# Row sums by half tiles, an early second expert tile, and group loads on the weights' queue, in a streaming-encoder block with a product-key expert layer

## What is computed

```python
qry = (xt @ w_query).reshape(TOKEN_BLOCK, PEER_HEADS, 2, PEER_HALF)
s1 = einsum('thd,hnd->thn', qry[:, :, 0], sub_keys1); s2 = ...   # top 16 of each, then top 16 of their sums
gate = softmax(top_s, axis=-1)
u, vv = expert_down[idx], expert_up[idx]
pre = einsum('td,thkd->thk', xt, u)
act = gelu(pre) * gate
out = einsum('thk,thkd->td', act, vv)
```

## Time and profile before

| | us |
|---|---|
| median of 3 runs | 3568.76 (3567.64 to 3570.26) |
| profiled execution, its own time | 3564.6 |
| its span | 3562.8 |
| TensorE busy (matmuls) | 3507.9, 98% |
| TensorE's weight loads busy | 3183.2, 89% |
| VectorE busy | 2171.1, 61% |
| ScalarE busy | 1413.8, 40% |
| POOL busy | 2045.6, 57% |

### The profile page before, as it was taken

One profiled execution on the slowest core, in us unless ns is written; L12 is line 12 of the kernel. 1 busy time (PEld: TensorE's weight loads), 2 busy tenths in 40 slices (PEclk: granted clock), 3 DMA queues, 4 the chain that ended last, 5 costly groups with the idle time before them and its releaser, 6 DMA issues.

```text
span 3562.8 us, 50874 instructions
## 1 busy us (share of the span) xinstructions
PE 3507.9 (98%) x20053; PEld 3183.2 (89%) x20053; DVE 2171.1 (61%) x3773; ACT 1413.8 (40%) x1780; POOL 2045.6 (57%) x718
## 2 busy tenths in 40 slices
PE   7999999999999999999999999999999999999999
PEld 5777777777788888898999999999999999999999
DVE  6333434343685137897676767443577777777774
ACT  5544545555422223323444444433333333333332
POOL 2333333333344434377666667687777777777774
PEclk9999999999999999999999999999999999999999
DMA  4322222222344332288999898999999999999994
GB/s 153 134 105 101 94 88 96 83 99 85 119 142 180 119 114 95 92 312 347 346 364 350 345 366 348 355 380 385 379 375 370 361 373 365 387 371 366 370 368 167
DMA packets 184738, 895.04 MB, mean 251 GB/s; under 512 B 15720, under 2 KB 69224, under 8 KB 90600
## 3 DMA queue, kind: packets, MB, share of 16 engines
q1 hardware_dynamic: 59232, 399.47, 30.1%
q0 software_dynamic: 49392, 359.68, 25.5%
q10 hardware_dynamic: 75928, 133.30, 10.2%
HBM read 828.39 MB, written 69.21 MB: 252 GB/s over the span
## 4 chain that ended last, share of the span: by engine, by line
PE 59%; issue 22%; DVE 8%; POOL 6%; DMA 3%; ACT 1%; DVEq 0%; ACTq 0%; POOLq 0%; SPq 0%
PE ps L1524 56%; DVE ps L1309 6%; POOL w_lo L350 5%; PE ps L1754 2%; DMA expert_rows<-down_rows,idx 1%; DVE h_dense L1442 1%; DMA w_e_raw<-w_stream 1%; POOL w_e_lo L357 1%; DVE expert_rows L1296 0%; PE ps L1688 0%; DMA g_dram<-gate_buf 0%; DVE hn_lo L1139 0%; POOL expert_rows L385 0%; ACTq L847 0%; ACT w_e_hi L724 0%
## 5 line engine op out<-in xcount | busy, mean ns | idle before, releaser
L357 POOL TENSOR_TENSOR w_e_lo<-w_e_raw,w_e_hi 128x2048 fp32r<-128x2048 f32 x256 | 1184.5, 4628 | 476.4 <-ACT w_e_hi L724 474.9
L350 POOL TENSOR_TENSOR w_lo<-w_raw,w_hi 128x2048 fp32r<-128x2048 f32 x115 | 536.6, 4666 | 934.2 <-ACT w_hi L417 934.2
L1524 PE MATMUL ps<-sn_hi,w_e_hi 128*128 128x344 f32 x2048 | 664.2, 324 | 11.4 <-POOL w_e_lo L357 8.7
L1524 PE MATMUL ps<-act_hi,w_e_hi 128*128 128x344 f32 x2048 | 658.4, 321 | 11.4 <-DVE h_dense L1442 11.4
L1524 PE MATMUL ps<-sn_lo,w_e_hi 128*128 128x344 f32 x2048 | 655.3, 320 | 0.0
L1524 PE MATMUL ps<-act_hi,w_e_lo 128*128 128x344 f32 x2048 | 655.2, 320 | 0.0
L1524 PE MATMUL ps<-sn_hi,w_e_lo 128*128 128x344 f32 x2048 | 654.1, 319 | 0.0
L1524 PE MATMUL ps<-act_lo,w_e_hi 128*128 128x344 f32 x2048 | 651.5, 318 | 0.0
L724 ACT ACTIVATE w_e_hi<-w_e_raw 128x2048 fp32r<-128x2048 f32 x256 | 489.2, 1911 | 191.3 <-DMA w_e_raw<-w_stream 106.6
L1296 DVE SCALAR_TENSOR_TENSOR expert_rows<-expert_rows,ps 128x2048 f32<-128x2048 f32 x171 | 388.3, 2282 | 259.7 <-DMA expert_rows<-down_rows,idx 143.2
L1524 PE MATMUL ps<-xn_hi,w_hi 128*128 128x512 f32 x1088 | 447.2, 411 | 18.7 <-DVE xn_lo L927 18.7
(11 more groups left out here) (260 smaller groups left out, 4853.7 us busy)
## 6 DMA issues: line engine op xcount, KB each, us to landing
w_e_raw<-w_stream SPq DMA_DIRECT2D x256, 1024.0 KB
w_raw<-w_stream SPq DMA_DIRECT2D x116, 1024.0 KB, 4.8
gel_dram<-gel_all ACTq DMA_DIRECT2D x32, 704.0 KB
g_dram<-gate_buf ACTq DMA_DIRECT2D x11, 2048.0 KB
gel_in<-gel_dram ACTq DMA_DIRECT2D x32, 704.0 KB
g_exp<-g_dram ACTq DMA_DIRECT2D x32, 704.0 KB
gate_dram<-g_raw ACTq DMA_DIRECT2D x32, 256.0 KB, 2.0
g_in<-gate_dram ACTq DMA_DIRECT2D x16, 512.0 KB, 5.8
```

The source lines that it names most:

```text
L350: nc.gpsimd.tensor_tensor(wlo[s][:, :], raw[s][:, :], whi[s][:, :].bitcast(F32), ALU.subtract).then_inc(lo_ready, 1)
L357: nc.gpsimd.tensor_tensor(e_lo[j % 4][:, :], e_raw[j % 4][:, :], e_hi[j % 3][:, :].bitcast(F32), ALU.subtract).then_inc(lo_ready, 1)
L1524: m = mm(ps[:, bank, 0:width], lhs[:, w], r, start=(n % (3 * per) == 0), stop=(n % (3 * per) == 3 * per - 1))
```

## The change

1. `FIRST_USED` gets six other numbers.
2. Items are placed by half tiles (`ITEM_HALF`); the tile of each item is as before. VectorE does a tile's rows in two places, one for each half; in the up stage each quarter of a group has the same order, and the fourth low part comes behind the row of that quarter's first half.
3. `peer_hi(1)` moves right behind `peer_hi(0)`, ahead of the last but one query block's key scores; `query_out` of the last block moves between the ninth and tenth `scaled_hi`; POOL waits for all of `sn_lo` before `low(1)` and not behind `low(2)`.
4. `gates(n)` and `gates_out(n)` stand a tile later, `one_hots(n)` where it was.
5. `load_group` of groups 2 to 31 moves from ScalarE's queue to SP's, behind the load of tile 4g + 3 of each group.

```diff
-FIRST_USED = [5, 9, 11, 14, 16, 18]
+FIRST_USED = [6, 10, 13, 16, 19, 21]
...
-ITEM_TILE = [T_GATES + (i - FIRST_ROWS) * DOT_TILES // (ADD_X - FIRST_ROWS) if i < ADD_X
-             else T_ACT + 1 + (i - ADD_X) * ADD_TILES // (N_ITEMS - ADD_X)
+ITEM_HALF = [2 * T_GATES + (i - FIRST_ROWS) * 2 * DOT_TILES // (ADD_X - FIRST_ROWS) if i < ADD_X
+             else 2 * T_ACT + 2 + (i - ADD_X) * 2 * ADD_TILES // (N_ITEMS - ADD_X)
              for i in range(FIRST_ROWS, N_ITEMS)]
+ITEM_TILE = [k // 2 for k in ITEM_HALF]
...
+            sp_view = g_dram.rearrange("g p (k c) -> p g k c", c=4 * GT)
+
+            def load_group(g):
+
+                s = slot_of(g)
+                sp.wait_ge(gel_out[g % 2], 16 * (g // 2 + 1))
+                sp.wait_ge(up_in[s], 32 * (loads_of(g) - 1))
+                sp.dma_start(gel_in[s][:, :], gel_dram[g]).then_inc(up_in[s], 16)
+                sp.dma_start(g_exp[s][:, :].rearrange("p (g c) -> p g c", g=GATE_GROUPS),
+                             sp_view[:, :, bass.ds(g, 1), :].rearrange("p g k c -> p (g k) c")).then_inc(up_in[s], 16)
+
             for j in range(2 * EXPERT_TILES):
                 load_experts(j)
+                g = (j - EXPERT_TILES - 3) // 4
+                if j >= EXPERT_TILES and j % 4 == 3 and g + 2 < GROUPS:
+                    sp.wait_ge(a_lo, 4 * g + 4)
+                    load_group(g + 2)
...
             for t in range(2 * EXPERT_TILES):
+                if t == 0:
+                    pool.wait_ge(slo_ready, CT)
                 if t + 1 < 2 * EXPERT_TILES:
                     low(t + 1)
                 if t == 1:
                     pool.wait_ge(idx3_ready, 1)
-                    pool.wait_ge(slo_ready, CT)
...
                     if isinstance(t, int) and t == CT - 2:
                         peer_hi(0)
+                        peer_hi(1)
...
             key_out(CT - 2)
-            peer_hi(1)
             for c in range(CT):
                 scaled_hi(c)
-            query_out(CT - 1, 1)
+                if c == CT // 2:
+                    query_out(CT - 1, 1)
             key_out(CT - 1)
...
-                    if GATE_TILE[n] == t:
+                    if GATE_TILE[n] + 1 == t:
                         gates_out(n)
...
-                    if g + 2 < GROUPS:
-                        if g:
-                            act.wait_ge(a_lo, 4 * g + 4)
-                        load_group(g + 2)
...
-            def rows_of_tile(t):
+            def rows_of_half(k):
                 for i in range(FIRST_ROWS, N_ITEMS):
-                    if tile_of(i) == t and i != TURN_X:
+                    if ITEM_HALF[i - FIRST_ROWS] == k and i != TURN_X:
...
+                rows_of_half(2 * t)
                 k = t - T_FIRST - 3
                 if 0 < k <= 4:
                     low(k - 1, 0, k - 1)
...
-                rows_of_tile(t)
+                rows_of_half(2 * t + 1)
...
+                for q in range(4):
+                    add_dense(g, 4 * q)
+                    if g + 1 < GROUPS:
+                        product(n + q, q)
+                    add_dense(g, 4 * q + 1)
+                    rows_of_half(2 * (t + q))
+                    add_dense(g, 4 * q + 2)
+                    if g + 1 < GROUPS:
+                        low(n + q, s, q)
+                    add_dense(g, 4 * q + 3)
+                    rows_of_half(2 * (t + q) + 1)
...
-                          for k, n in enumerate(n for n in range(N_GATES) if GATE_TILE[n] == t)}
+                          for k, n in enumerate(n for n in range(N_GATES) if GATE_TILE[n] + 1 == t)}
```

More of the change, by code:

```diff
@@ L1460, in _ @@
                 s, n, t = 1 - g % 2, 4 * g + 4, EXPERT_TILES + 4 * g
[L1461 to L1477, removed]
-                    low(n + 1, s, 1)
-                add_dense(g, 7)
-                add_dense(g, 8)
-                if more:
-                    product(n + 2, 2)
-                add_dense(g, 9)
-                rows_of_tile(t + 2)
-                add_dense(g, 10)
-                if more:
-                    low(n + 2, s, 2)
-                add_dense(g, 11)
-                add_dense(g, 12)
-                if more:
-                    product(n + 3, 3)
-                add_dense(g, 13)
-                if more:
-                    low(n + 3, s, 3)
-                add_dense(g, 14)
-                rows_of_tile(t + 3)
-                add_dense(g, 15)
+                for q in range(4):
[9 more added lines that the diff above has]
+                    rows_of_half(2 * (t + q) + 1)
                 if t <= T_SPARSE_OUT < t + 4:
```

## The result

| | before | after |
|---|---|---|
| median of the runs, us | 3568.2 (3563.04 to 3570.26, 4 runs) | **3623.21** (3618.12 to 3626.74, 4 runs) |
| profiled execution, own time | 3564.6 | 3621.58 |
| its span | 3562.8 | 3619.8 |
| mean granted clock of TensorE | 0.997 | 0.989 |

What follows compares the result with a forecast made beforehand. TensorE was taken as nearly never idle, so only its gaps could be won. Terms 31.0 - 3.0 - 14.2 + 3 = +16.8 on 3564.6 gave 3581.4; 4.2 more for the median gave 3585.6, range 3572 to 3618.

Steps and rivals of the forecast that it cites:

- Start, -5.8: Start of the down stage: early second tile, undisturbed sn_lo and earlier q_sb gain 5.8 us; tile 1 waits 1.6.
- The list: Down stage, tiles 14 to 21: later gather places leave it 31.0 us behind, the start's 5.8 us gain included.
- 16.5, 7.1 and 19.4: Forecast TensorE waits in us at tiles 16, 17 and 21, each for a row product or what hangs on it.
- 17.15 us: Down stage: time from first of four gathers to start of last row's product, used twice; with 12.6 the lag is 21.9.
- Rival 3: Tiles 14 to 21: gather places don't decide, VectorE's own sorting does; faster, 3546 us, chance 0.08.
- Gates a tile behind, -3.0: Down stage: gate products a tile later remove two waits behind one-hots, -3.0 us, between 0 and -4.4.
- Halves, -14.2: Up stage: row sums by half tiles remove 44 stops (-23.9 us), late low parts add 9.7; net -14.2, between -23.9 and 0.
- 22 stops of 0.44 us behind act_lo: Up stage, group starts: last low part of activations behind a row is 0.44 us late in 22 of 31 groups, +9.7.
- Rival 2: Up stage: halves gain nothing because another wait replaces the 44 stops; +14.2 us, 3600 us, chance 0.10.
- Group loads on the weights' queue, +3: Up stage: weight tiles land later behind 1.4 MB of group loads; +3 us taken, between 0 and 37.
- Rival 1: Up stage: weights behind group loads make each of 31 groups end 1.2 to 1.5 us later; +37, 3620 us, chance 0.15.
- about 21 us: Up stage: latest landing of weight tile 4g+4 after its group's start that was held early enough for the activations.

Runs made afterwards that it cites:

- e4: The kernel before with the new list of gather places alone: 3619.56 us (ratio 1.0155).
- e12: e2 with the softmax exponential at tile 16 instead of 14: 3580.5 us (ratio 1.0039).
- e6: e3 with the gate products and their copies back in the tile of their one-hots: 3546.54 us (ratio 0.9951).
- e3: The changed kernel with the old list of gather places and the group loads back on ScalarE's queue: 3548.02 us (ratio 0.9959).
- e5: e3 with each group's fourth low part placed ahead of the row of the first half again: 3540.07 us (ratio 0.9932).
- e2: The changed kernel with the group loads of gates and gelu results back on ScalarE's queue: 3585.44 us (ratio 1.0057).
- e1: The changed kernel with the old list of gather places: 3578.93 us (ratio 1.0044).
- e13: e1 with groups 2 to 31 filling the gates' table from the gelu results, same bytes in pieces of 5632 bytes instead of 512: 3550.14 us (ratio 0.9958).

## Why the prediction was wrong, and where it was right

By the terms of its sum. The profiled execution is 40.2 us above the forecast for it (3621.58, forecast 3581.4): 12.9 of these arose by the end of the down stage, 27.3 in the up stage.

- **Start, -5.8: right.** Tiles 1 to 13 are 5.6 us earlier, and the wait left at tile 1 is 1.2 us (forecast 1.6).
- **The list: right in mechanism and nearly in size.** Stops of 18.2, 8.3 and 17.6 us were forecast as 16.5, 7.1 and 19.4, and the lag at the end of tile 21 of 33.3 as 31.0. The interval I was least sure of, 17.15 us from the first gather to the last product, was 1624.69 - 1606.60 = 18.1. Taking the list out gives 44 and 37 us; the working implied 31.0 + 5.8 = 36.8. Rival 3 (the places don't decide) is refuted by e4, and e12 shows that the exponential's place isn't the bound either.
- **Gates a tile behind, -3.0: wrong, by a later wait.** The stops behind one-hots fell as forecast, but e6 puts the whole at nothing, and in the change the lag grew by 7.6 us between tiles 22 and 127, 5.8 of them at tile 81, where ScalarE waits for the third store of gates (7.35 us, against 0.20). I had said that "the waits of ScalarE's copies stay". The third didn't: a tile later its store comes behind one of gelu results on the queue (e6).
- **Halves, -14.2: right, the size in part by luck.** e3's up stage is 21.7 - 6.3 = 15.4 us shorter in the profiled executions. The 44 stops behind h_dense went but for one. Forecast were 22 stops of 0.44 us behind act_lo; there were 22 with 10.2 us (0.46 each), and e5 takes them away. But the stops fell by 10.7 us in all (23.9 to 13.2), and the rest of the gain is TensorE's quicker pace, which no term had. Rival 2 fell.
- **Group loads on the weights' queue, +3: this is the step that failed.** It measured 38 (after less e2) and 31 (e1 less e3). Rival 1 had the size, at +37 and a chance of 0.15, but not the way: it had every group 1.2 to 1.5 us late. Two things were wrong in the working. I divided busy time by a share of the engines and took the one figure, 18.2 to 20.8 us from the group's start, for every group. The median was 20.8, the upper of the two, but the groups lay from 15.7 to 25.7, and 14 of 30 above 21. The limit of "about 21 us" fits: 7 of the 22 stops behind act_lo are over 1 us, 13.2 us together, and all of them follow a group with its tile at 20.9 or later. And I took bytes for the price where e13 shows that it is the pieces. What I quoted from the Trainium skill (DMA: Bandwidth & Descriptors, "Queues, rings and completion order") would have put the sum at the upper half of the bounds, and so it came; but the order in the ring alone doesn't make the price, since in e13 the weights stand behind the same bytes in the same order and lose nothing.
  The same section says that an engine changes from one queue row to another only between packets. The runs fit that but don't show it: if a queue with short packets gets no more turns than one with long ones, its bytes pass slowly, and the 704 KB in pieces of 512 bytes took 6.8 us from first to last piece, the same bytes in long pieces 3.5. How many pieces make a turn no run here shows.

The up stage thus took 16.1 us longer instead of 11.2 (14.2 - 3) less. The stops account for 9.2 of the 16.1 (33.1 us, 23.9 before). The rest is in the clock. Windows of the change, TensorE's granted clock among the columns (us, PE, PEld, DVE, ACT and POOL busy, PEclk, DMA share, GB/s):

```profile
2750.00:2850.00 100.00, 93.26 (x569) 92.13 (x568) 71.91 (x88) 37.57 (x42) 72.61 (x29) 0.97 0.91 346
...
2600.00:2700.00 100.00, 99.30 (x628) 98.73 (x628) 71.36 (x90) 35.86 (x39) 75.16 (x29) 1.00 0.98 379
```

After stops of 3.23, 2.28, 2.25 and 2.32 us the clock fell for a few us from full speed (2.4 GHz) to the lower level (1.2 GHz); after another of 2.28 us, at 3360, it didn't. 0.97 stood in five windows of 50 us of the up stage (the fifth, at 3560 to 3610, without such a stop), in which the kernel before had 1.00 everywhere: about 5 x 50 x 0.03 = 7.5 us, which no term of mine had.

## What to carry to other kernels

Before a load is put ahead of another on a queue, look at its pieces and not at its bytes alone: here a queue that shared the engines with others took twice as long over short pieces, and the weights behind them waited. And look at the spread of such a wait and not only at its middle: with a median just below the limit, the groups above it paid. A list of places that an in-order engine follows is a schedule for everyone behind it: moving a gather by one low part moved it by what that low part itself waits for, and the whole came to 37 to 54 us. Work that is moved by a tile takes its stores with it, to another place in a queue: e3 was 9.3 us ahead of e6 at tile 20, gave 6.6 back behind a store of gates, and 2.3 were left at the end of the stage. And stops that are taken away are worth their sum only if the engine's pace stays, as e3 and e5 show.

## What was not expected of the hardware

- The same 704 KB took 3.5 us from first to last piece in pieces of 5632 bytes and 6.8 in pieces of 512, on one queue, beside gathered rows.
- After stops of 2.25 to 3.23 us the granted clock was lower (0.97 from 2750 to 2850 us, which has two such stops).
- At full granted clock the products of the up stage start every 0.158 us or, for stretches, every 0.153.
- An issue can hold its engine for long. ScalarE's of a load of 688 KB, the next issue behind a group's loads, took 12.68 us in the change, and 10.64 in the kernel before; what held it isn't shown. The row of the change:

```profile
2493.17 12.68 ACTq L865 DMA_DIRECT2D h_dense<-h_dense_dram  x1
```
